# One-core decoder step: expert 0's rows from one-hot products instead of a DRAM round trip, router weights loaded elsewhere and earlier

## What is computed

```python
def moe(h, rw, rb, w1, w3, w2):
    t = h.reshape(-1, d)
    logits = t @ rw + rb
    top_v, top_i = lax.top_k(logits, TOP_K)          # 2 of 8 experts for each token
    gates = jax.nn.softmax(top_v, axis=-1)
    combine = jnp.sum(jax.nn.one_hot(top_i, N_EXPERTS) * gates[..., None], axis=1)
    for e in range(N_EXPERTS):
        out = out + combine[:, e:e + 1] * swiglu(t, w1[e], w3[e], w2[e])
```

## Time and profile before

| | |
|---|---|
| median of three runs | 1556.95 us (1556.41 to 1562.45) |
| the profiled execution | 1560.83 us, its span 1558.9 us |
| PE busy | 93% of the span |
| DVE, ACT, POOL busy | 30%, 13%, 8% |
| read from and written to HBM | 339.13 MB and 28.49 MB, 236 GB/s over the span |
| mean granted clock of TensorE | 0.951 |
| expert loop | from 1055.11 us to the end of its last product at 1526.36 us |

### The profile page before, as it was taken

One profiled execution on the slowest core, in us unless ns is written; L12 is line 12 of the kernel. 1 busy time (PEld: TensorE's weight loads), 2 busy tenths in 40 slices (PEclk: granted clock), 3 DMA queues, 4 the chain that ended last, 5 costly groups with the idle time before them and its releaser, 6 DMA issues.

```text
span 1558.9 us, 22150 instructions
## 1 busy us (share of the span) xinstructions
PE 1447.7 (93%) x9354; PEld 1003.0 (64%) x9354; DVE 469.1 (30%) x1300; ACT 206.3 (13%) x430; POOL 126.1 (8%) x156
## 2 busy tenths in 40 slices
PE   7999999999998999999997899849999999999991
PEld 5887677788776888878886776634444444444440
DVE  3345656520352211141397336120000000000003
ACT  2121112101211100000112221120000000000001
POOL 3003414300010200000000001020000000000001
PEclk9998889999998999999999998879999999999996
DMA  9743644645483994434443358736999999999962
GB/s 280 220 149 95 167 105 146 234 151 173 147 324 134 335 388 154 142 108 156 155 142 119 125 192 299 264 137 245 385 396 380 387 402 356 373 391 352 399 245 94
DMA packets 184056, 368.26 MB, mean 236 GB/s; under 512 B 8419, under 2 KB 117243, under 8 KB 183808
## 3 DMA queue, kind: packets, MB, share of 16 engines
q1 hardware_dynamic: 162600, 292.47, 52.7%
q0 software_dynamic: 19264, 71.23, 13.2%
q10 hardware_dynamic: 2096, 3.15, 0.6%
HBM read 339.13 MB, written 28.49 MB: 236 GB/s over the span
## 4 chain that ended last, share of the span: by engine, by line
PE 87%; DVE 7%; DMA 3%; issue 2%; POOL 1%; ACT 1%; SPq 0%; ACTq 0%; POOLq 0%; DVEq 0%
PE psum L886 32%; PE psum L1426 13%; PE psum L1298 10%; PE psum L1432 6%; PE psum L1465 6%; PE psum L1195 5%; PE psum L1471 3%; DVE arena L2198 2%; DMA ring<-in_cache_mem_v_dram 1%; PE psum L1237 1%; PE psum L1262 1%; PE psum L1229 1%; PE psum L911 1%; DMA expert_rows<-arena 1%; PE psum L1443 1%
## 5 line engine op out<-in xcount | busy, mean ns | idle before, releaser
L886 PE MATMUL psum<-hT,ring 128*128 128x264 f32 x1168 | 276.2, 399 | 1.1 <-ACT hT L1508 1.1
L886 PEld LDWEIGHTS psum<-hT,ring 128*128 128x128 f32 x1168 | 228.1, 196 | 49.1 <-issue 6.9
L886 PE MATMUL psum<-arena,ring 128*128 128x264 f32 x992 | 229.2, 395 | 9.3 <-ACT arena L1669 5.0
L886 PEld LDWEIGHTS psum<-arena,ring 128*128 128x128 f32 x992 | 192.9, 195 | 44.1 <-ACT arena L1669 5.4
L1298 PE MATMUL psum<-hT,ring 128*128 128x264 f32 x704 | 157.0, 386 | 0.0
L1298 PEld LDWEIGHTS psum<-hT,ring 128*128 128x128 f32 x704 | 133.8, 190 | 22.9
L1426 PE MATMUL psum<-ring,arena 128*64 128x384 f32 (+1 forms) x704 | 137.2, 541 | 0.0
L1195 PE MATMUL psum<-ring,arena 128*128 128x256 f32 x512 | 115.9, 388 | 0.0
L1195 PEld LDWEIGHTS psum<-ring,arena 128*128 128x128 f32 x512 | 99.2, 195 | 19.3 <-issue 5.3
L1791 DVE TENSOR_TENSOR arena<-psum,rstd 128x264 f32<-128x264 f32 (+3 forms) x117 | 43.8, 393 | 214.4 <-PE psum L1298 118.8
L1426 PEld LDWEIGHTS psum<-ring,arena 128*64 128x64 f32 x704 | 49.1, 137 | 79.9 <-issue 79.9
(11 more groups left out here) (432 smaller groups left out, 1227.4 us busy)
## 6 DMA issues: line engine op xcount, KB each, us to landing
ring<-in_moe_w_dram SPq DMA_DIRECT2D x72, 1024.0 KB, 17.2
arena<-in_moe_w_dram SPq DMA_DIRECT2D x40, 1024.0 KB, 15.0
ring<-in_moe_w_dram SPq DMA_DIRECT2D x44, 768.0 KB, 16.3
ring<-in_ffn_w_dram SPq DMA_DIRECT2D x30, 1024.0 KB, 5.4
ring<-in_w_in_even_dram SPq DMA_DIRECT2D x22, 1024.0 KB, 5.9
ring<-in_cache_mem_k_dram POOLq DMA_DIRECT2D x16, 1024.0 KB, 8.2
ring<-in_cache_mem_v_dram POOLq DMA_DIRECT2D x16, 1024.0 KB, 6.4
arena<-in_moe_w_dram SPq DMA_DIRECT2D x20, 768.0 KB, 17.3
```

Of the source, the lines that this page charges most:

```text
L886: ins = mm(outs_[m][0:mw, 0:T], wv[:, k, m * mw:(m + 1) * mw], rhs(base + k), start=(base + k == 0), stop=(kc == len(chunks) - 1 and k == ...
```

## The change

Two edits. First, expert 0's rows no longer come from DRAM. DVE builds `chosen0`, a matrix of tokens by 96 rows with a one where a token picked expert 0 and has that slot. PE multiplies `htok` with it, 24 products in three token blocks (128, 128 and 8 tokens), into the same PSUM banks that `turn_rows` filled. The scatters stay, since all later experts read from `expert_rows`; SP no longer loads block 0 ahead of the loop, so each count of `rows_in` is lower by 16. Second, `rwt` and `rbt` move in `arena` behind `fss`, and POOL clears and loads them behind the eviction of the pooling products (`taken(pool, ("pw", OT - 1))`; ACT, 1663), ahead of its loads of layer 1's memory cache. The final norm's gain keeps its place on POOL and gets a semaphore of its own.

```diff
         back = (htok, fin)
-        rwt = R.take(KT, 32)
-        rbt = R.take(NE)
         lgT = R.take(T)
...
         fss = R.take(3, 1)
+        rwt = R.take(KT, 32)
+        rbt = R.take(NE)
+        chosen0 = view(SLOT, 3, CAP)
...
             sp.wait_ge(sem("rows_out"), 96)
-            rows_load(0)
             sp.wait_ge(sem("rounds_known"), 1)
...
             memory_k_out(1)
+            taken(pool, ("pw", OT - 1))
+            nc.gpsimd.memset(rwt[:, :, :], 0.0).then_inc(sem("blank_set"), 1)
+            pool.wait_ge(sem("blank_set"), 2)
+            load(rwt[:, :, 0:NE], w["router_w"][0].rearrange("(t p) e -> p t e", p=P), "router_in")
+            load(rbt, w["router_b"].to_broadcast([P, NE]), "router_in")
             more_kv(1)
             taken(pool, ("xo1", KT - 1))
             pool.wait_ge(sem("kst"), 32)
             pool.wait_ge(sem("vst"), 32)
-            nc.gpsimd.memset(rwt[:, :, :], 0.0).then_inc(sem("blank_set"), 1)
-            pool.wait_ge(sem("blank_set"), 2)
-            load(rwt[:, :, 0:NE], w["router_w"][0].rearrange("(t p) e -> p t e", p=P), "router_in")
-            load(rbt, w["router_b"].to_broadcast([P, NE]), "router_in")
-            load(fgain, w["norm_final"].unsqueeze(0).to_broadcast([P, DM]), "router_in")
+            load(fgain, w["norm_final"].unsqueeze(0).to_broadcast([P, DM]), "fgain_in")
...
-            pe.wait_ge(sem("router_in"), 48)
+            pe.wait_ge(sem("router_in"), 32)
...
-            pe.wait_ge(sem("rows_in"), 16)
-            turn_rows()
+            pe.wait_ge(sem("chosen0_ready"), 1)
+            for j in range(2):
+                for t in range(4):
+                    for c in range(3):
+                        n = P if c < 2 else NB
+                        ins = mm(psum[:, (5, 2)[j], t * CAP:(t + 1) * CAP], htok[0:n, c, (4 * j + t) * P:(4 * j + t + 1) * P],
+                                 chosen0[0:n, c, :], start=(c == 0), stop=(c == 2), skip_group_check=True)
+                if j == 0:
+                    ins.then_inc(sem("turned_low"), 1)
+            ins.then_inc(sem("rows_turned"), 1)
...
-                    pe.wait_ge(sem("rows_in"), n * 16 + 32)
+                    pe.wait_ge(sem("rows_in"), n * 16 + 16)
...
-            dve.wait_ge(sem("router_in"), 48)
+            dve.wait_ge(sem("router_in"), 32)
...
             step(v.tensor_tensor(slot[:, :, :], slot[:, :, :], over[:, 0, :, :], ALU.add))
+            for c in range(3):
+                n = P if c < 2 else NB
+                ins = v.tensor_scalar(chosen0[0:n, c, :], const("iota")[0:n, :], slot[0:n, c, 0:1], picked[0:n, c, 0:1],
+                                      ALU.is_equal, ALU.mult)
+            ins.then_inc(sem("chosen0_ready"), 1)
             v.tensor_tensor(first[:, :, :], first[:, :, :], slot[:, :, :], ALU.mult)
...
-            dve.wait_ge(sem("router_in"), 48)
+            dve.wait_ge(sem("fgain_in"), 16)
             combine(0)
```

## The result

| | before | after |
|---|---|---|
| median | 1559.58 us (6 runs, 1556.41 to 1562.45) | 1550.76 us (6 runs, 1547.67 to 1552.73) |
| ratio, 95% interval | | 0.9943, 0.9927 to 0.996 |
| span of the profiled execution | 1558.9 us | 1549.0 us |

The change saves some 9 us, 0.57%: faster, but by half of the 17.7 us forecast, and 1550.76 lies above the range. Part of the miss of the range is the base: the three runs of the kernel before that the prediction started from had a median of 1556.95, six have 1559.58. The larger part is in the trace.

A forecast was written before the change was run, and what follows sets the result against it. PE was busy 93% of the span, so only its idle or low-clock stretches could pay. Reaching the loop 15.3 us earlier plus 2.4 in its first block gave 17.7 saved, 1556.95 to 1539.2 us; range 1535 to 1548.

The forecast's parts named there:

- Router loads: PE's wait ahead of the router's products is for three loads; issuing two earlier on POOL saves 8.6 us.
- Transposes ahead of the rank: Token transposes no longer delay the rank products, which start once experts are chosen: 1.9 us more saved.
- The matrix: Building the matrix of ones and zeros puts three DVE operations ahead of the row numbers, costing 0.8 us.
- The new wait for ACT's evictions: Before the new products PE waits for ACT's last token eviction, which ends last, at 1031.7 us.
- The products: The 48 instructions that build expert 0's rows on PE take 7.3 us; bounds 5.1 and 10.6 us.
- Into the loop: From the end of gathering expert 0's rows to the expert loop's first product: 0.83 us, kept as before.
- First block: The expert loop's first 32 product instructions run at the full clock instead of the lower one, saving 2.4 us.
- Queues: SP's later row loads and weight refills are not delayed: no cost, by a margin of some 10 us.
- The rival of the low clock: Clock stays low through the gather: 48 instructions take 10.6 us, 13.3 us saved, or 10.9 with slow first block; chance 0.20.
- two arguments against it: Against a low clock: 8-row products stand between full ones; the clock rose at 1036.0 after 5.3 us of transposes alone.
- the first wait was not the loads: PE's wait before the router's products has another cause; only the gather part pays, 3.5 to 8.5 us; chance 0.05.
- the weight stream would take the gain back: Weight loading sets the expert loop's end, so PE starts earlier only to wait: 1553 to 1557 us; chance 0.04.

The follow-up runs named there:

- padded run: The changed kernel with the third token block filled with zeros from 8 to 128 rows: 1541.14 us, ratio 0.9883 to the kernel before.
- grouped: The changed kernel with its 48 instructions reordered, the 8-row ones together at the end of each half: 1543.75 us, ratio 0.9899 to the kernel before.
- 32-row runs: The changed kernel with the third token block padded to 32 rows: 1550.02 us, ratio 0.9935 to the kernel before.
- last padded run: The changed kernel padded to 128 rows, two token transpose groups moved ahead of the rank products, ACT's exponential behind the evictions: 1541.86 us, ratio 0.9883.
- last experiment: The kernel before, with the final norm's gain on its own semaphore and the router's products waiting only for weights and bias: 1559.81 us, executed once.

## Why the prediction was wrong

Point by point, each from the end of the output product:

- *Router loads*, forecast 8.6 us: the router's products end 1.77 behind it instead of 10.32, **8.55**. Right.
- *Transposes ahead of the rank*, 1.9 more: rank begins 7.51 behind it instead of 17.77, so 10.26 in all against 10.5. Right.
- *The matrix*, 0.8: 0.80. The new wait for ACT's evictions: they end at 1032.82, 13.71 behind the output product, forecast 13.5. Right, and the chain names ACT as what releases the gather.
- *The products*, forecast 7.3 us, upper bound 10.6: **11.20**, above the bound. This is the step that failed. The prices came from lines 1043 and 1138, all of whose products have 128 rows, and the products with 8 rows were priced as if that made no difference. For 48 equal products those prices were good: 0.116 us each in the padded run, against 0.122. What they lack is the price of the turns between unequal products, which the grouped and 32-row runs show: 0.159 each at the full clock, and a clock that then falls.
- *Into the loop*, 0.83: 0.83. *First block*, forecast 2.4 saved: 9.78 instead of 9.44, 0.34 lost. The step behind it, that PE comes out of 48 products at the full clock, failed with the products: the gather hands the loop the lower clock. It holds where the turns are gone (7.09).
- *Queues*, no cost: as the lines of POOL and SP show. The expert loop has no new waits.

The shortfall of the stage and first block, forecast 17.7 against (36.91 + 9.44) - (25.98 + 9.78) = 10.6, is 7.1 us: 3.9 in the products, 2.7 in the first block, and the rest in the small differences ahead. In the padded run the medians differ by 18.8 us, close to the sum that the forecast made for products at the full clock.

The rival of the low clock, at 0.20, came nearest, and with both of its parts it gave 10.9 saved. That the two numbers are so close is in part luck: it had 48 instructions in 10.6 us at the lower clock throughout, while the gather began at 1.00 and lost time by its turns even there, and the ranks began about when forecast (7.5 us behind the output product, forecast 7.3). Its argument, the 8-row products of the earlier trace rows, pointed the right way but is another case. Those products (line 1237) follow each other with none of 128 rows between, and from 941.27 on, in the later part of that stretch at 0.50, the products are line 1195's with 128 rows. Of the two arguments against it, the first was the wrong way round: that 128-row products stand between the 8-row ones does not help, it is part of the cost. The second, the rise of the clock at 1036.0 after transposes, says nothing of products with unequal rows.

On transposes themselves the runs bear that second reading out. In the padded run PE ran nothing but transposes from 1025.91 to 1030.42; the clock was 0.61 on mean from 1026.00 to 1029.50 and 1.00 from 1030.50. In the last padded run a stretch with 48 of them was at 1.00 from end to end. The Trainium skill (TensorE: Matmul & The Clock Gate, Part 4: PE-mode transpose) says that the full clock does not engage for transposes, which do not count as busy in the same way; these traces, in float32, do not agree. The same page calls transpose mode four times faster for float data (Terms). Here the factor was about two: with 128 columns a product took 2 x 0.125 us, a transpose 2.84/24 = 0.118.

That the first wait was not the loads, and that the weight stream would take the gain back, fell: the first by the last experiment, the second because the padded run starts its loop over 15 us earlier than before and keeps all of it.

## What to carry to other kernels

Before products replace a transfer, look at the shapes of neighbours in PE's order, not only at their count: a small remainder block that comes round in every tile cost 5.6 us of 11.2 here, some of it by a lower clock that the code behind inherited, and filling the block up with zeros to full rows gave both back. When a change of two parts gains about what one part should, run each part alone: here one had all of it, and the other had traded a wait for work of the same length. A wait put down to "issue" is worth checking against the landing times of the loads on the same semaphore.

## What the runs showed that had not been expected

- Products with 128 and with 8 rows in turn took 0.159 us an instruction at the granted clock of 1.00, with 128 and 32 rows the same 0.159; all with 128 rows took 0.116. With the same products in an order of 3 turns instead of 15 it was 0.126.
- In all three kernels with such turns at every tile the granted clock fell from 1.00 to 0.50 in the middle of the gather, while PE had no idle time, and did not come back before the loop's first block; in the four others with this gather it stood at 1.00 through the gather in the profiled execution.
